# Chunk weights on ScalarE's DMA queue, up-projection weights stored one block per column tile

## What is computed

```
h    = rms_norm(x) * (1 + scale1) + shift1            # D_MODEL = 1024
q, k, v, u, vg = split(h @ w_in)
cat  = concat(stick_breaking(q, k, v), spatial_gate(u, vg))
x    = x + gate1 * (cat @ w_out)                      # w_out  1024 x 1024
h2   = rms_norm(x) * (1 + scale2) + shift2
up   = h2 @ w_up                                      # w_up   1024 x 5632, two halves of 2816
conv = conv_b + sum(conv_w[i] * up shifted by i)      # width 3, causal
x    = x + gate2 * ((silu(conv_g) * conv_v) @ w_down) # w_down 2816 x 1024
```

## Time and profile before

| what | us |
|---|---|
| median of 3 runs | 3850.82 (3850.78 to 3855.89) |
| the profiled execution, device time | 3855.71 |
| its span | 3853.9 |
| start of `finish_layer`'s first DMA | 1286.26 |
| first matmul of chunk 1, 2, 3, 4 | 1302.36, 1904.84, 2500.68, 3094.08 |
| first matmul of the sample chunk's output projection | 3702.78 |
| last matmul | 3848.20 |

### The profile page before, as it was taken

The page is one execution under the profiler, slowest core; times in us unless marked ns, Lnnn a source line. Parts: engine busy times, 40 slices in busy tenths (PEclk is TensorE's granted clock), DMA queues, the critical chain, the costliest instruction groups (busy, mean ns, idle before and its releaser), DMA issues.

```text
span 3853.9 us, 54699 instructions
## 1 busy us (share of the span) xinstructions
PE 3559.7 (92%) x16996; PEld 2064.5 (54%) x16996; DVE 1731.4 (45%) x2719; ACT 1051.3 (27%) x2114; POOL 1083.5 (28%) x957
## 2 busy tenths in 40 slices
PE   5799999989999689999989999999999989999978
PEld 1344444456565257763357774347774437775333
DVE  1121221178788256552256652246653245663222
ACT  0222222189889022220022220012220012221011
POOL 0001010156566035540025450015541014551000
PEclk8899999999999799999999999999999999999977
DMA  7411211111100557567757657757667666666668
GB/s 286 172 47 33 68 31 33 27 65 45 46 12 2 177 143 200 158 193 207 239 144 191 184 158 215 213 175 197 173 186 213 183 208 170 189 173 188 184 202 253
DMA packets 482109, 576.43 MB, mean 150 GB/s; under 512 B 29482, under 2 KB 289778, under 8 KB 479196
## 3 DMA queue, kind: packets, MB, share of 16 engines
q1 hardware_dynamic: 477116, 555.89, 49.7%
q10 hardware_dynamic: 4704, 17.04, 1.1%
HBM read 538.02 MB, written 34.81 MB: 149 GB/s over the span
## 4 chain that ended last, share of the span: by engine, by line
PE 51%; DMA 5%; SPq 4%; issue 3%; DVE 3%; POOL 1%; ACT 1%; DVEq 0%; POOLq 0%; ACTq 0%
PE ff_pB L1464 24%; PE ff_pB L1415 21%; PE s_pZ L1003 3%; DMA ff_w<-in_w_up 3%; PE s_pO L1017 2%; SPq L954 2%; SPq L962 1%; DMA ff_w<-in_w_down 1%; DMA s_kpage<-in_cache_k 1%; DVE s_kT L1105 1%; SPq L964 1%; PE s_pZ L1009 0%; PE ff_pB L1429 0%; PE ff_pB L1476 0%; SPq L1331 0%
## 5 line engine op out<-in xcount | busy, mean ns | idle before, releaser
L1415 PE MATMUL ff_pB<-ff_w,ff_hidden 128*128 128x512 f32 (+1 forms) x1496 | 669.0, 599 | 9.7 <-DMA ff_w<-in_w_down 5.0
L1464 PE MATMUL ff_pB<-ff_act_in,ff_w 128*128 128x256 f32 x2112 | 516.1, 388 | 47.0 <-DMA ff_w<-in_w_up 35.6
L1814 POOL TENSOR_TENSOR ff_sums<-ff_w 128x512 f32<-128x512 f32 x88 | 116.7, 1326 | 1330.8 <-DMA ff_w<-in_w_up 1130.5
L1464 PEld LDWEIGHTS ff_pB<-ff_act_in,ff_w 128*128 128x128 f32 x2112 | 402.8, 193 | 127.9 <-issue 63.6
L1415 PEld LDWEIGHTS ff_pB<-ff_w,ff_hidden 128*128 128x128 f32 (+1 forms) x1496 | 269.8, 186 | 372.5 <-issue 357.8
L450 PE MATMUL in_pA<-in_w,in_hT 128*128 128x512 f32 (+1 forms) x1024 | 449.1, 594 | 1.0 <-DVE in_hT L569 1.0
L1105 DVE STREAM_TRANSPOSE s_kT<-s_kpage 128x1024 f32<-128x1024 f32 x256 | 309.8, 1229 | 198.2 <-DMA s_kpage<-in_cache_k 118.9
L1758 DVE SCALAR_TENSOR_TENSOR ff_conv<-ff_raw,k_vecT,ff_conv 128x512 f32<-128x512 f32 (+1 forms) x440 | 392.7, 892 | 7.8
L889 POOL TENSOR_TENSOR at_stop<-at_stop,at_left 128x512 f32<-128x512 f32 (+3 forms) x320 | 311.5, 999 | 181.5 <-ACT at_stop L829 175.6
L1464 PE MATMUL ff_pB<-ff_diff,ff_sums 128*128 128x256 f32 x1408 | 336.6, 382 | 8.5 <-DVE ff_diff L1701 5.5
L450 PEld LDWEIGHTS in_pA<-in_w,in_hT 128*128 128x128 f32 (+1 forms) x1024 | 186.4, 185 | 231.9 <-issue 230.7
(11 more groups left out here) (201 smaller groups left out, 4074.1 us busy)
## 6 DMA issues: line engine op xcount, KB each, us to landing
s_kpage<-in_cache_k SPq DMA_DIRECT2D x512, 256.0 KB, 3.8
s_vpage<-in_cache_v SPq DMA_DIRECT2D x512, 256.0 KB, 3.1
ff_w<-in_w_up SPq DMA_DIRECT2D x220, 512.0 KB, 6.0
ff_w<-in_w_down SPq DMA_DIRECT2D x70, 768.0 KB, 5.0
wada<-in_w_ada SPq DMA_DIRECT2D x8, 3072.0 KB, 12.3
ff_w<-in_w_out SPq DMA_DIRECT2D x20, 1024.0 KB, 6.3
in_w<-in_w_in SPq DMA_DIRECT2D x5, 2048.0 KB, 18.6
in_x<-in_x_prompt SPq DMA_DIRECT2D x16, 512.0 KB, 5.7
```

The costliest lines, as they stand in the source:

```text
L1415: last = pe.matmul(pB[t][0:R, :], src, w[:, n % RING, i * 512:i * 512 + 512], start=kt == 0, stop=kt == nk - 1)
L1464: last = pe.matmul(into, left[:, kt * P:(kt + 1) * P], right[:, kt, :], start=kt == 0 and p in (1, 2, 5), stop=kt == KT // 2 - 1, skip_gro ...
```

## The change

There are two parts.

1. Who issues the weight loads of the prompt chunks. `wait_used` and `load_w` move out of SP's block and take the engine as an argument. SP's program for the prompt chunks keeps only the page loads and `act_in`. ACT issues loads 0 to 2 of the first chunk ahead of its loads of x; in `body`, the new function `loads_after` says after which event of the plan each load comes: load (n + 3) % 42 right after the last event that reads load n. At the end of a chunk these are loads 0 to 2 of the next one, those of the sample chunk too. From load 3 on, the sample chunk's loads stay on SP.
2. The layout of w_up. The host hands over w_up rearranged as 22 blocks of 128 rows of 2048 floats (`column_tiles`), so that a tile is one DMA of 128 rows of 8 KB. The semaphore counts follow: every load now adds 16.

```diff
+def loads_after(plan):
+    last_use = {load_of(event): at for at, event in enumerate(plan) if event[0] in ("tok", "mul")}
+    follow = {}
+    for n, at in last_use.items():
+        follow.setdefault(at, []).append((n + RING) % LOADS)
+    return follow
...
+        def load_w(eng, c, nt, n):
+            wait_used(eng, c, nt, n - RING)
+            slot = w[:, n % RING, :]
+            def dma(dst, src):
+                eng.dma_start(dst, src).then_inc(w_loaded[n % RING], 16)
...
+            elif n < WO + UP:
+                dma(slot, a["w_up"][n - WO])
...
-                    elif n < WO + UP:
-                        f = n - WO
-                        for half in range(2):
-                            src = a["w_up"][0].rearrange("(r p) n -> p r n", p=P)[:, :, half * DFF + f * P:half * DFF + (f + 1) * P]
-                            dst = slot[:, half * D:(half + 1) * D].rearrange("p (r n) -> p r n", r=KT)
-                            load_w(n, dst, src)
...
             order = load_order(plan_p)
+            order = [x for x in order if x[0] != "w"]
...
-            loads(NCH, load_order(plan_s), 1)
+            loads(NCH, [x for x in load_order(plan_s) if x[0] == "w" and x[1] >= RING], 1)
...
             def body(c, R, nt, W, plan):
-                for kind, *which in plan:
+                follow = loads_after(plan) if R == P else {}
+                for at, (kind, *which) in enumerate(plan):
...
+                    for n in follow.get(at, ()):
+                        load_w(act, c + (n < RING), TT, n)
                 for t in range(nt):
                     store_y(c, R, nt, t)
+            for n in range(RING):
+                load_w(act, 0, TT, n)
             load_x(0, P, TT, first=True)
...
+def column_tiles(w_up):
+    return w_up.reshape(KT, P, 2, FT, P).transpose(3, 1, 2, 0, 4).reshape(FT, P, 2 * D)
...
+    inputs["w_up"] = column_tiles(np.asarray(inputs["w_up"]))
```

More of the change, by code:

```diff
@@ L1301, in tok, with wait_used @@
             return 4 * TT * c + (2 * phase + n2) * nt + t + 1
+        def wait_used(eng, c, nt, n):
+            if n < 0:
+                c, nt, n = c - 1, TT, n + LOADS
+            if WO <= n < WO + UP and nt == 1:
+                eng.wait_ge(up_part, n - WO + 1)
+            elif WO <= n < WO + UP:
+                eng.wait_ge(up_done, NUP * c + UP_AT[n - WO, 4])
+            elif n in (1, 3, WO + UP + 7, WO + UP + 15):
+                phase, n2 = int(n >= WO + UP), int(n in (3, WO + UP + 15))
+                eng.wait_ge(tok_done, tok(c, phase, n2, nt - 1, nt) + 4 * TT)
+            else:
+                at = n // 2 + 1 if n < WO else 2 + (n - WO - UP) - (n - WO - UP) // 8 + 1
+                eng.wait_ge(w_used, 16 * c + at + 16)
+        def load_w(eng, c, nt, n):
[3 more added lines that the diff above has]
+                eng.dma_start(dst, src).then_inc(w_loaded[n % RING], 16)
+            if n < WO:
+                n2, kq = n // 2, n % 2
+                src = a["w_out"][0].rearrange("(r p) n -> p r n", p=P)[:, 4 * kq:4 * kq + 4, n2 * 512:n2 * 512 + 512]
+                dma(slot.rearrange("p (r n) -> p r n", r=4), src)
+            elif n < WO + UP:
+                dma(slot, a["w_up"][n - WO])
+            else:
+                d = n - WO - UP
+                n2, f = d // 8, d % 8 * DF
+                nf = min(DF, FT - f)
+                src = a["w_down"][0].rearrange("(r p) n -> p r n", p=P)[:, f:f + nf, n2 * 512:n2 * 512 + 512]
+                dma(slot[:, 0:nf * 512].rearrange("p (r n) -> p r n", r=nf), src)
         plan_p, plan_s = chunk_plan(TT, step_pieces()), chunk_plan(1, [])
@@ L1341, in loads @@
                         continue
[L1342 to L1348, removed]
[L1349 to L1360 removed]
+                    load_w(sp, c, nt, *which)
             load_in(0, P)
             order = load_order(plan_p)
+            order = [x for x in order if x[0] != "w"]
             with sp.Fori(0, NCH - 1) as c:
@@ L1389, in loaded @@
             def loaded(c, n):
-                per = 16 * LOADS // RING + 16 * sum(1 for q in range(WO, WO + UP) if q % RING == n % RING)
-                before = sum(2 if WO <= q < WO + UP else 1 for q in range(n % RING, n + 1, RING))
-                pe.wait_ge(w_loaded[n % RING], per * c + 16 * before)
+                pe.wait_ge(w_loaded[n % RING], 16 * (LOADS // RING) * c + 16 * (n // RING + 1))
             def project(c, R, nt, phase, n2, q, t):
@@ L1807, in weight_sums @@
                 n, at = WO + f, 4 * (FT * c + f)
-                per = 16 * LOADS // RING + 16 * sum(1 for q in range(WO, WO + UP) if q % RING == n % RING)
-                landed = sum(2 if WO <= q < WO + UP else 1 for q in range(n % RING, n + 1, RING))
                 A11, A12, A21, A22, S2, S3, S4 = weights_of(f)
-                pool.wait_ge(w_loaded[n % RING], per * c + 16 * landed)
+                pool.wait_ge(w_loaded[n % RING], 16 * (LOADS // RING) * c + 16 * (n // RING + 1))
                 if f >= 2:
```

21 lines of the change are left out of this document (removed).

## The result

| | us |
|---|---|
| kernel before, median of 4 runs | 3853.36 (3850.78 to 3855.91) |
| changed kernel, median of 4 runs | 3801.03 (3800.15 to 3806.38) |
| ratio | 0.9867, 95% interval 0.985 to 0.9884 |
| profiled execution: span | 3804.6 (before 3853.9) |

The change gains 52 us by the medians and 49.3 by the spans. Forecast were 84.0 and a time of 3767, with a range up to 3798: the sign is right, the time lies outside the range. Two executions were slow, one of 4123 us in the experiment with the start held and one of 6031 us of the kernel before beside it, at granted clocks of 0.85 and 0.56 where all others had 0.95 to 0.97, and they are in no median, ratio or gain of this text.

The account below looks back on a forecast made before the run. PE, busy 92%, was taken as the bound, with late weight loads from SP's order and the sample chunk's transfer rate. 60.7 + 5.3 + 14.4 + 2.0 + 1.6 = 84.0 us off 3850.8 gave 3767; range 3748 to 3798.

Parts of the forecast that it names:

- the eight stalls: PE's waits for up-projection weights in the prompt chunks, two per chunk: all 35.6 us go, plus 16.4 of slow clock.
- That ACT can issue without anybody waiting: Prompt chunks: 42 added issues per chunk stay hidden; rival that issues block ACT: 3903 us, chance 0.05.
- That the layout brings rate: Sample chunk's up-projection: tile period 3.60 to 2.80 us, 14.4 gained; rival of no rate: 3783 us, chance 0.12.
- What is late next? PE itself.: Prompt chunks after the stalls go: PE runs back to back, nothing else late; 55.0 us forecast for four up-projections.
- The same bytes pass today through one queue in front of the same pages.: Argument against the rival that weight loads on the second queue delay key pages, which was put at 52 us.
- the collision: Rival: weight tiles hold up key pages, twenty of 64 steps wait 2.6 us each; 52 us lost, 3819 us, chance 0.07.
- 5.7: Prompt chunks' four down-projections: 4.0 us of weight stalls and 1.7 of slow clock behind the longest were to go.
- The start: Start of the block: first matmul 3.3 us earlier and 2 off the 4.38 us key wait; 5.3 gained, bounds 0 and 10.
- The turn: Last prompt chunk to sample chunk: ACT issues w_out loads 0 to 2 earlier, 1.6 us gained of a 2.83 wait.
- The wait for `gate_s` has its own chain on SP and stays: Ahead of the sample chunk's output projection: this wait was to stay unchanged.
- tile 3's stall: Sample chunk's up-projection: 2 us of this 3.43 us stall were to go through an earlier, shorter load.
- it came back to the full clock after each prompt stall when it had no gap: Sample chunk: reason for expecting a higher PE clock once data came every 2.63 us; period taken as 2.80.

Follow-up runs that it names:

- the experiment with the start held: Changed kernel, but at the start ACT issues load 0, then waits for the first key pages before loads 1, 2 and x: 3787.91 us, ratio 0.9818.
- the queue alone: Changed kernel with ACT's queue kept but w_up in its old layout, two DMAs per tile: 3823.29 us, ratio 0.9910.
- the layout alone: Kernel before the change with w_up in blocks, one DMA per tile, all loads on SP: 3841.83 us, ratio 0.9959.
- swapping POOL's order: Changed kernel, but POOL does tile f-1's gated product ahead of tile f+1's weight sums: 3784.44 us; the same swap in the kernel before: 3819.39 us.

## Why the prediction missed

**Right.** That SP's order makes the eight stalls, not the transfer: the queue alone removes all of them, the layout alone leaves 32.1 of 35.6. That ACT can issue without anybody waiting: its w_up issues took 0.334 us in the median and 0.367 at most, and PE's wait for ACT's copy of product 6 appears nowhere. The start's first matmul, 3.5 us earlier, counted from the block's first DMA, against 3.3. That the layout brings rate, in the main in the sample chunk: 12.8 us there with the layout alone and 13.2 in the changed kernel, against 16.4; the rest of the layout's 15.8 fits the 3.5 us by which the stalls became shorter, which the prediction put at nothing. One reading was off by a little: from the late load's issue to PE it is 8.1 us, not 7.5.

**"What is late next? PE itself."** This step of the up-projections failed: 55.0 forecast, 46.2 gained. I had looked at what PE waits for around the stalls, and not at what an earlier tile starts on POOL. Its sums fall on DVE's taps, 1058 to 1141 ns each, and PE's waits for DVE's sum into `raw` rose by 6.3 us. That is 6.3 of the 8.8; swapping POOL's order gives back 17 us, since it removes the older part of the interference as well. The small rest I did not trace.

**"The same bytes pass today through one queue in front of the same pages."** This was the reason against the collision, and it is wrong. The earlier trace rows itself shows the weight load behind the pages, not in front of them. In the down-projections SP issued w_down behind its value pages and never while it issued key pages; ACT's loads now run beside the key pages, and these take 6.9 us instead of 4.2 from the last issue to the transpose. The four key waits grew from 5.2 to 13.8 us, and together with the clock behind some of them (twelve matmuls took 7.35 us behind the 3.83, and 5.32 at the same place before) the stage gave -6.4 instead of 5.7. Putting w_down back leaves two of them, with 0.9 us.

**The start.** I compared only what the first matmul needs, and took 2 us of the key wait as gained because no w_out stands between the pages any more. But ACT now asks for 3 MB of w_out and 2 MB of x at once, of which the first matmul needs 1 MB. The first key wait became 9.51 instead of the 2.4 that I had left of it; the start gave -0.1 instead of 5.3, and -0.9 counted from the block's first DMA. Holding ACT back brings the wait to 1.21. By the Trainium skill ("DMA: Bandwidth & Descriptors", Queues, rings and completion order) each DMA engine takes turns between the queues that have work for it. The turns themselves are in no trace here; what fits them are three places, here, in the down-projections and at the turn, where SP's transfers came later while ACT's were in flight and came sooner once those loads were held or moved.

**The turn.** "The wait for `gate_s` has its own chain on SP and stays": it does have its own chain, but of short transfers, and they share the engines with three weight loads and the y stores. It went from 9.3 to 14.0; SP's wait for the store of `catT` ahead of it from 1.4 to 6.2. The 2.83 for w_out became 1.05, now for DVE's copies; the stage gave -2.9 instead of 1.6.

**The sample chunk.** The rate came nearly as estimated, 359 to 378 GB/s for 399, and tile 3's stall fell from 3.43 to 1.19 us. What failed is "it came back to the full clock after each prompt stall when it had no gap". Here, from 3710.29 to 3733.17, PE had no gap and stayed at 1.2 GHz, 2.86 us a tile, more than the data's pace at 395 GB/s (2.65); only then was the full clock granted, and the next wait for a load, 2.09 us, ended it. A period of 3.005 instead of 2.80 costs 3.7 us. At the full clock, with two wide matmuls more, the period is 2.73.

Why the clock stayed low so long is open. In the prompt chunks the stationary tile has 128 columns and here it has 32 (128*32 in the rows), but that alone does not explain it: the changed kernel's down-projection of the same chunk has 32 too, with 512 moving columns instead of 256, and ran at

```profile
3762.00:3778.00 16.00, 16.00 (x38) 3.95 (x36) 0.00 (x0) 0.00 (x0) 0.00 (x0) 1.00 0.76 252
```

That added wide matmuls bring the full clock is shown; the same number of narrow ones was not tried.

**The range** ended at 3798, 3 us short. The collision stood in the rivals as one mishap of 52 us with a chance of 0.07; it came as a small effect in three places at once. In the sum the same three places stood as +5.3, +5.7 and +1.6, and they were -0.1, -6.4 and -2.9: 22.0 us of the 34.7 that the spans lack. The up-projections and the sample chunk are 8.8 and 3.2 more.

## What to carry to other kernels

Before a load is moved to a second queue, list what is in flight on the first at that moment, and weigh the stall that the move ends against what it will delay: the stalls for w_down were 5.0 us in all, and moving it cost 15 net. Here w_up alone on the second queue was worth 18 us more than all weights. When a transfer comes earlier, follow what it starts on the other engines; an engine that nobody waits for can still slow one that somebody waits for. And do not count on the full clock as soon as PE has no gap: here it came 23 us later.

## What the runs showed of the hardware

- A DVE tap of 128x512 on f32 took 0.77 us while POOL stood still and 1.7 beside POOL's sums. In the prompt chunks the mean moved from 1141 to 862 ns by POOL's order alone, worth 17 us in the changed kernel and 36 in the kernel before (by the medians).
- With matmuls of 32 stationary and 256 moving columns, and the small ones that fold their results, the granted clock was 0.50 for 24 us with PE busy for 23.7 of them, and 1.00 in the 4.5 us behind. With 32 stationary and 512 moving columns it was 1.00 over 16 us. With two or four matmuls of 128 stationary and 256 moving columns added per tile it was 1.00 over 50 and 58 us. Two of them gave 3792.85 us against 3801.03, four 3809.53.
- Rows of 8 KB moved at 351 (layout alone, 3736 to 3790) to 395 GB/s in the stage where pieces of 512 B of the same tensor, whose rows lie 22.5 KB apart, moved at 291.
- Key pages of 256 KB each became ready 6.9 us after the last issue with weight loads in flight on the other queue, 4.2 without (first down-projection).
